# Where two pieces of a projection stand in TensorE's order at a change of head

## What is computed

```python
q, k, v = jnp.split(h @ w_in, 3, axis=-1)
q = rms_norm(q.reshape(B, S, H, 2, Dh), q_g)
k = rms_norm(k.reshape(B, S, H, 2, Dh), k_g)
...
    s = jnp.where(mask, s, -jnp.inf)       # chunk-causal, chunks of 64
    p = jax.nn.softmax(s, axis=-1)
    pd = (p[:, :, 0] - lam * p[:, :, 1]).astype(v.dtype)
    return jnp.einsum('bhqs,bshe->bqhe', pd, v)
```

## Time and profile before

| | |
|---|---|
| median of 3 runs | 2810.46 us |
| profiled execution | 2813.27 us, span 2811.5 us |
| mean granted TensorE clock | 0.992 |
| TensorE busy | 2724.1 us, 97% of the span |
| DVE, ACT, POOL busy | 1897.5, 1502.1, 1077.5 us |
| attention with its first projections | about 0 to 1535 us; the MLP follows |

### The profile page before, as it was taken

The page is one execution under the profiler, slowest core; times in us unless marked ns, Lnnn a source line. Parts: engine busy times, 40 slices in busy tenths (PEclk is TensorE's granted clock), DMA queues, the critical chain, the costliest instruction groups (busy, mean ns, idle before and its releaser), DMA issues.

```text
span 2811.5 us, 42849 instructions
## 1 busy us (share of the span) xinstructions
PE 2724.1 (97%) x14784; PEld 2371.3 (84%) x14784; DVE 1897.5 (67%) x2726; ACT 1502.1 (53%) x2987; POOL 1077.5 (38%) x956
## 2 busy tenths in 40 slices
PE   7999999999999999979999899999999999999999
PEld 7998989989898999967887678888888888888887
DVE  6777787777778787775776666555555555666655
ACT  5666666666666666664454434344444444344443
POOL 5633334243333424341000344444443444444443
PEclk9999999999999999989999999999999999999999
DMA  8742424243242423224445996666667976666663
GB/s 270 264 136 93 154 96 162 91 145 112 97 150 96 150 96 133 93 90 139 168 173 191 352 345 238 236 236 264 267 240 283 353 285 234 233 234 238 237 236 131
DMA packets 181808, 544.09 MB, mean 194 GB/s; under 512 B 14736, under 2 KB 88208, under 8 KB 136592
## 3 DMA queue, kind: packets, MB, share of 16 engines
q1 hardware_dynamic: 180016, 541.25, 52.7%
q10 hardware_dynamic: 1632, 0.79, 0.1%
HBM read 470.81 MB, written 71.17 MB: 193 GB/s over the span
## 4 chain that ended last, share of the span: by engine, by line
PE 83%; issue 6%; DVE 4%; ACT 3%; DMA 2%; POOL 1%; SPq 0%; ACTq 0%; POOLq 0%; DVEq 0%
PE banks L2163 21%; PE banks L2139 21%; PE banks L421 16%; PE banks L666 5%; PE banks L563 4%; PE banks L565 4%; PE banks L638 4%; PE banks L825 3%; PE banks L668 2%; PE banks L513 2%; ACT pt_hi L647 1%; ACT p_all L605 1%; DVE mx L582 1%; DMA u<-u_factors 1%; DVE p_all L627 1%
## 5 line engine op out<-in xcount | busy, mean ns | idle before, releaser
L2139 PE MATMUL banks<-u,w 128*128 128x512 f32 x2688 | 615.4, 390 | 8.2 <-DMA u<-u_factors 6.5
L2139 PEld LDWEIGHTS banks<-u,w 128*128 128x128 f32 x2688 | 506.0, 188 | 114.7 <-issue 8.0
L421 PE MATMUL banks<-w_hi,u_ring 128*128 128x384 f32 x2048 | 589.1, 347 | 11.2 <-DVE u_ring L1315 4.6
L2163 PE MATMUL banks<-w,a_hi 128*128 128x512 f32 x1792 | 552.1, 389 | 1.5 <-issue 1.0
L1905 POOL TENSOR_TENSOR w<-w_raw,w 128x1024 fp32r<-128x1024 f32 x96 | 245.2, 2569 | 558.5 <-ACT w L1954 283.4
L605 ACT ACTIVATE p_all<-banks,bias 128x1024 f32<-128x1024 f32 (+7 forms) x384 | 332.0, 867 | 182.8 <-DVE bias L585 116.4
L2163 PEld LDWEIGHTS banks<-w,a_hi 128*128 128x128 f32 x1792 | 336.2, 188 | 72.2 <-issue 2.3
L421 PEld LDWEIGHTS banks<-w_hi,u_ring 128*128 128x128 f32 x2048 | 375.8, 188 | 15.8 <-issue 9.9
L2163 PE MATMUL banks<-w,a_lo 128*128 128x512 f32 x896 | 348.7, 389 | 0.0
L451 POOL TENSOR_TENSOR qk_rs<-qk_var,minus_half 128x4 f32<-128x4 f32 x128 | 129.6, 1012 | 563.0 <-DVE qk_var L445 563.0
L421 PE MATMUL banks<-w_lo,u_ring 128*128 128x384 f32 x1024 | 344.4, 336 | 0.0
(11 more groups left out here) (151 smaller groups left out, 4731.9 us busy)
## 6 DMA issues: line engine op xcount, KB each, us to landing
u<-u_factors SPq DMA_DIRECT2D x224, 1024.0 KB, 9.5
u_ring<-u_scratch SPq DMA_DIRECT2D x112, 1024.0 KB, 5.3
w_raw<-in_mlp_w SPq DMA_DIRECT2D x128, 512.0 KB, 6.6
u_scratch<-u_ring SPq DMA_DIRECT2D x16, 1024.0 KB, 5.0
u_factors<-q_hi SPq DMA_DIRECT2D x23, 512.0 KB, 4.3
u_factors<-q_lo SPq DMA_DIRECT2D x23, 512.0 KB, 4.4
w_raw<-in_a_w_in SPq DMA_DIRECT2D x90, 128.0 KB, 4.6
p_all<-in_x SPq DMA_DIRECT2D x16, 512.0 KB, 5.8
```

The source lines that it names most:

```text
L421: last = pe.matmul(proj[:, 0:3 * HD], u[:, part, kt, :], w[:, kt, :], start=(kt == 0 and part == 0 and w is w_hi), stop=(kt == KT - 1 and ...
L2139: last = pe.matmul(banks[:, UP_BANKS[p] + f, :], w[:, 2 * k2 + k, f * P:(f + 1) * P], u[:, :, part, k, :], start=(STARTS[p] and k2 == 0 an ...
L2163: last = pe.matmul(banks[:, DOWN_BANKS[p] + t, :], a[:, p % 2, f, t * P:(t + 1) * P], b[:, f, :], start=(STARTS[p] and f == 0 and a is a_h ...
```

## The change

In `first_step` of TensorE's stream the first quarter of the projection's second half moves from behind the second group's value products to behind the second turning, and the last quarter moves from behind the third group's value products to ahead of them, behind the last turning. Nothing else is touched; no other engine's stream changes.

```diff
             pe_turn_p(pe, a - 1, 0)
             pe_turn_p(pe, a - 1, 1)
+            if n < ALL:
+                pe_project(pe, n, 1, (0,))
             pe_values(pe, a - 1, 0)
             pe_turn_p(pe, a - 1, 2)
             pe_values(pe, a - 1, 1)
-            if n < ALL:
-                pe_project(pe, n, 1, (0,))
             pe_turn_p(pe, a - 1, 3)
-            pe_values(pe, a - 1, 2)
             if n < ALL:
                 pe_project(pe, n, 1, (1,))
+            pe_values(pe, a - 1, 2)
             pe_values(pe, a - 1, 3)
```

## The result

The changed kernel takes 2834.33 us (median of 6 runs, 2830.89 to 2835.68) against 2811.28 us before (6 runs beside it, 2808.08 to 2813.52): +23.0 us. The ratio is 1.0077, with a 95% interval of 1.0067 to 1.0086, so it is slower by more than the 0.2% that can be told from no change, and the forecast of 2835.1 us is 0.8 us off.

What follows compares the result with a forecast made beforehand. TensorE, 83% of the chain that ended last, was taken as the bound. Per head 2.0 us of wait plus 2.1 of low clock make 4.1, six times 24.6, on 2810.46: 2835.1 us, range 2822 to 2842.

Steps and rivals of the forecast that it cites:

- The wait: Behind turning 1, the first piece waits for POOL's low weights (L400) until about 273.87, leaving TensorE idle 3.8 us.
- Full-clock cost, 2.0 us per head: First step of each of six heads: last value product gives way at 280.4 instead of 278.40, nothing else late.
- The clock, 2.1 us per head, between 1.8 and 3.0: Matmuls behind the wait run at half rate for 4.5 us (3.9 to 6.5), 0.46 us per low microsecond.
- the case of 1518: Attention step of the earlier trace: after 2.62 us idle at 1518.06 the clock stayed low some 3.9 us.
- Second piece at nothing: Second piece moved ahead of values 2: ends 0.9 us earlier, costed at nothing, at most 0.6 us at stake.
- The wait for L432: TensorE's wait for ACT's copy before the next step's first projection: claimed to stay 0.6 us.
- Rival (a): Six heads: the wait comes but no lower clock, 6 x 2.0 = 12 us, 2822.5; chance 0.13.
- Rival (b): Behind turning 1: low weights ready by about 270, piece fills the idle time, 7 us gained, 2803.4; chance 0.04.
- The break-even of 271.9: First of the six steps: start of the first piece at which the move neither gains nor loses, 278.40 - 6.5.
- Rival (c): Inside the head: 0.9 us wait taken back, clock kept, weights some 0.5 us earlier; costs 4 us, 2814; chance 0.03.
- the 0.9 us before a score: TensorE's idle time before a score at a change of head, 0.9 us, which one rival had taken back.
- Grows by nothing else: Stretch between two heads, 160.5 us from step to step: claimed to grow by the same 4 us only.

Runs made afterwards that it cites:

- the kernel that keeps TensorE busy: Changed kernel plus 32 identity transpositions into a free bank between turning 1 and the first moved piece: +12.4 us against the kernel before, ratio 1.0045.
- the first alone: Changed kernel with the second piece back behind values 2, only the first moved behind turning 1: +25.5 us against the kernel before, ratio 1.0090.
- POOL out of the way: Changed kernel with POOL's low products of pieces 2 and 3 cut to 6 of 768 columns: -7.2 us against the kernel before, ratio 0.9971.
- own weights: Changed kernel, but each moved piece waits only for the weight piece it reads: +1.5 us against the kernel before, ratio 1.0006.

## Why the prediction was right, point by point

- **The number.** 0.8 us off is better than the method. Runs of one kernel lie 5 us apart, and two things cancelled: the cost was forecast at 24.6 us and measured at 23.0, and the median before, taken again with six runs, lies 0.8 us higher than the one the forecast was added to.
- **The wait.** "It starts at about 273.87": it starts at 273.95, or 273.88 on the clock of the trace before. The wait is POOL's, and it follows the end of POOL's product in five kernels. This is shown.
- **Full-clock cost, 2.0 us per head.** 2.1 by the kernel that keeps TensorE busy. It holds because nothing behind the piece is late; ACT and DVE waited longer, not TensorE. That the low halves stay hidden, as the prediction said for turning 2 with the second piece in between, is owed to the two moves together: with the first alone values 2 wait 0.3 us at three heads.
- **The clock, 2.1 us per head, between 1.8 and 3.0.** A little too high. In the profile after, the way from the first piece to the next projection is 11.12, 10.03, 10.02, 9.98, 9.91 and 9.81 us at the six heads; less 8.45 that is 2.7 us at the first and 1.4 to 1.6 at the others, 1.7 on average, and the medians give 1.8. My lower end of 1.8 was above five of the six. What was wrong is the length, not the price: with work on the engine the clock was low for 5.8, 3.4, 3.4, 3.4, 3.2 and 3.0 us, and 0.46 us for each of these gives 2.7, 1.6, 1.6, 1.6, 1.5 and 1.4. I had counted the 3.9 us of the case of 1518 from the end of the wait, but its clock was still up for the first half microsecond, so it was low for 3.4 us:

```profile
1517.00:1518.50 1.50, 0.44 (x4) 0.42 (x4) 1.39 (x3) 0.91 (x2) 0.00 (x0) 1.00 0.19 74
1518.50:1521.50 3.00, 2.95 (x11) 2.38 (x10) 2.17 (x4) 1.20 (x2) 0.00 (x0) 0.51 0.86 318
```

And 4.5 us was a choice between two cases. The trace before has three more long waits that I did not use, 3.88, 3.28 and 3.41 us at 1247.07, 1254.09 and 1261.25; at each the clock was at 0.50, and behind the last for 4.7 us. The sum by what was measured is 6 x (2.1 + 1.7) = 22.8. The Trainium skill ("TensorE: Matmul & The Clock Gate", HAM oscillation) would have given an estimated 0.8 us per head from its 1.67 us throttled; the trace does not agree with that size, since its low stretches lasted 3.4 us and more, and the cost lies between the two values, nearer mine.
- **Second piece at nothing.** So it is by itself, +0.3 us; beside the late first piece it hides the 0.3 us at three heads that were shown above. The wait for L432 is 0.6 us in every kernel.
- **Rival (a), no lower clock**, would have been 2822.5; the kernel that keeps the clock up gives +12.4 us, which is what (a) would have looked like. In the change the clock did fall, so (a) is refuted.
- **Rival (b), the hole is filled**, was wrong for this kernel but right in its arithmetic: with POOL out of the way the gain is 7.2 us, forecast 7. The break-even of 271.9 stands to 0.1 us (280.22 - 8.45 = 271.8): own weights starts at 271.63, which is 272.1 by the time of the trace before, and costs 0.3 us per head in its rows where the clock stays up, +1.5 us in its median.
- **Rival (c)**: the 0.9 us before a score stayed 0.9 us; nothing was taken back. "Grows by nothing else" was right for the heads; the later difference I take for the chance of single executions.

## What to carry to other kernels

An idle gap on the busiest engine can be filled only with work whose inputs are there at that moment: before moving a piece ahead, read the producer's timeline on the other engine for the waits that go with it, and work out the start from which the move breaks even. Here the wait was 0.2 us from binding in its old place, a sign that the place had no room in front of it; splitting a wait for two products into one for each, and moving one producer ahead, turned a loss of 23 us into a gain of 6.5 us by the rows and 10 by the medians. Where a wait of some microseconds on TensorE can't be avoided, count some of the matmuls behind it at half rate, here 1.4 to 2.7 us more behind 3.8 us of idle time. Extra transpositions into an unused bank kept the clock up here and were worth their place.

## What the hardware showed that was not expected

- The low clock behind a gap is not a fixed price. At the six heads, after 3.8 and 5.7 us of idle time it came every time (12 of 12, in two kernels, and 6 of 6); after 2.4 us at three of six, in turn; after 2.0 us at one of six; and after 1.31 us at one of 18, in three kernels. With 2.4 us the steps that kept the clock and those that lost it had the same idle time to 0.01 us, and differed by 1.6 us behind it.
- The length of the low stretch differed too, behind one and the same idle time of 3.79 us: in the change it was 6.8 us at the first head, of which 1.0 us lay in the idle time, and 3.4 us at the other five; with the first piece alone it was 6.8 us at two heads and 3.4 us at four.
- In the change, the clock was in part still high when the work began again, and fell a microsecond into it: at the second head the first matmul behind the gap is a short one, and the granted clock of the stretches behind it is 1.00 and then 0.53.

```profile
439.18 0.41 PE L421 MATMUL banks<-w_hi,u_ring 128*128 128x384 f32 x1 [3.79 <-issue]
```

```profile
439.00:440.00 1.00, 0.82 (x5) 0.85 (x6) 0.00 (x0) 0.00 (x0) 0.79 (x3) 1.00 0.00 0
440.00:443.00 3.00, 3.00 (x16) 3.00 (x15) 0.00 (x0) 0.00 (x0) 0.00 (x0) 0.53 0.00 0
```

- POOL stands nearly still beside DVE's combination of probabilities (L627, 2.35 us from 266.59 in the trace before, two inputs from SBUF). The norm behind the factor begins at 267.15, so 1.8 us of it run beside the combination, and takes 2.69 us there and 1.04 us elsewhere; put the low product in its place and that takes 3.58 instead of 1.80 us and the norm is back at 1.04. Both lose 1.7 to 1.8 us, whichever instruction stands there. No run was made without the combination. The Trainium skill ("GPSIMD Engine Reference", Specifications) says that POOL shares its SBUF interfaces with VectorE and contends with instructions of two SBUF inputs; the trace agrees: nearly all of the 1.8 to 1.9 us in which the two ran beside each other were lost.
